# Scores and value products of two heads issued in turn on opposite halves of the array

## The reference

```python
s = einsum('bnqhgd,bnkhd->bnhgqk', qb, kk) * HEAD_DIM**-0.5      # sliding, n = block
s = where(valid, s + bias, NEG); p = softmax(concat([s, sink]))[..., :-1]
o = einsum('bnhgqk,bnkhd->bnqhgd', p, vv)

s = einsum('bqhd,bkhd->bhqk', q[:, q0:q1], k[:, :q1]) * HEAD_DIM**-0.5   # forgetting, block n
s = s + (c[:, :, q0:q1, None] - c[:, :, None, :q1])              # c: cumulative log of the gates
p = softmax(where(valid, s, NEG)); out = einsum('bhqk,bkhd->bqhd', p, v[:, :q1])
merged = sigmoid(ga) * (oa @ w_pa) + sigmoid(gb) * (ob @ w_pb)
```

## Time and profile before

| what | value |
|---|---|
| runs | 1684.04, 1686.79, 1687.28 us; median 1686.79 |
| profiled execution | 1683.52 us, span 1681.3 us from the first to the last instruction |
| granted TensorE clock | 0.994 of full |
| busy: PE, DVE, ACT, POOL | 1633.2, 1341.1, 735.2, 455.5 us |
| sliding steps, to the first forgetting scores | end at 224.83 us |
| first forgetting scores to the first product after the attention loop | 224.83 to 342.67 us |

### The profile page before, as it was taken

One profiled execution on the slowest core, in us unless ns is written; L12 is line 12 of the kernel. 1 busy time (PEld: TensorE's weight loads), 2 busy tenths in 40 slices (PEclk: granted clock), 3 DMA queues, 4 the chain that ended last, 5 costly groups with the idle time before them and its releaser, 6 DMA issues. The chain is left out here.

```text
span 1681.3 us, 26829 instructions
## 1 busy us (share of the span) xinstructions
PE 1633.2 (97%) x9808; PEld 1509.0 (90%) x9808; DVE 1341.1 (80%) x2856; ACT 735.2 (44%) x1288; POOL 455.5 (27%) x314
## 2 busy tenths in 40 slices
PE   5999999999799999999999999999999999999996
PEld 4897776678688899999999999999999999999996
DVE  4534455646568899999999989768899999899898
ACT  3314444443253344667666754444333333333331
POOL 0000000000001023333133342333554555457540
PEclk9999999999899999999999999999999999999998
DMA  4461111023234478899899999999999999999991
GB/s 147 121 198 57 42 50 39 13 84 95 85 99 148 134 251 302 275 353 327 276 311 346 331 347 320 368 406 362 405 404 407 407 409 407 407 407 406 407 404 77
DMA packets 185441, 438.47 MB, mean 261 GB/s; under 512 B 17832, under 2 KB 102000, under 8 KB 182880
## 3 DMA queue, kind: packets, MB, share of 16 engines
q1 hardware_dynamic: 73872, 227.43, 37.1%
q0 software_dynamic: 44080, 161.06, 26.0%
q10 hardware_dynamic: 67360, 48.28, 8.7%
HBM read 380.57 MB, written 56.13 MB: 260 GB/s over the span
## 5 line engine op out<-in xcount | busy, mean ns | idle before, releaser
L469 PE MATMUL psS<-hT_lo,hi 128*128 128x368 f32 (+2 forms) x1464 | 503.1, 344 | 4.6 <-DVE hT_lo L1033 3.9
L460 DVE TENSOR_TENSOR lo<-raw,hi 128x1024 fp32r<-128x1024 f32 x323 | 394.4, 1222 | 132.8 <-ACT hi L456 124.8
L470 PE MATMUL psS<-hT_hi,lo 128*128 128x368 f32 (+2 forms) x1464 | 495.0, 338 | 0.0
L471 PE MATMUL psS<-hT_hi,hi 128*128 128x368 f32 (+2 forms) x1464 | 492.8, 337 | 0.0
L456 ACT ACTIVATE hi<-raw 128x1024 fp32r<-128x1024 f32 x323 | 339.8, 1053 | 160.5 <-PE psS L471 104.0
L578 POOL DMA_INDIRECT gat<-in_u_rows,idx x144 | 216.4, 1503 | 395.9 <-DVE gat L1207 214.6
L469 PEld LDWEIGHTS psS<-hT_lo,hi 128*128 128x128 f32 x1464 | 275.2, 188 | 28.7 <-issue 15.8
L471 PEld LDWEIGHTS psS<-hT_hi,hi 128*128 128x128 f32 x1464 | 275.5, 188 | 12.4
L470 PEld LDWEIGHTS psS<-hT_hi,lo 128*128 128x128 f32 x1464 | 275.2, 188 | 10.1
L578 POOL DMA_INDIRECT gat<-in_v_exp,idx x144 | 222.4, 1544 | 225.5 <-DVE gat L1207 141.6
L773 ACT ACTIVATE act_hi<-act_t 128x368 fp32r<-128x368 f32 x128 | 65.6, 513 | 275.9 <-DVE act_t L1258 265.0
(11 more groups left out here) (314 smaller groups left out, 2667.4 us busy)
## 6 DMA issues: line engine op xcount, KB each, us to landing
raw<-in_u_exp SPq DMA_DIRECT2D x128, 512.0 KB
raw<-in_v_exp SPq DMA_DIRECT2D x128, 512.0 KB
gelu_dram<-gelu ACTq DMA_DIRECT2D x128, 184.0 KB
gates_dram<-gates ACTq DMA_DIRECT2D x92, 256.0 KB
gel_in<-gelu_dram SPq DMA_DIRECT2D x128, 184.0 KB
raw<-in_w_merge SPq DMA_DIRECT2D x24, 512.0 KB
gate_even<-gates_dram SPq DMA_DIRECT2D x8, 1472.0 KB
gate_odd<-gates_dram SPq DMA_DIRECT2D x8, 1472.0 KB
```

The lines of the kernel that those rows point to most:

```text
L460: nc.vector.tensor_tensor(lo[:, n % RING, :], raw[:, n % RING, :], hi[:, n % RING, :].bitcast(F32), ALU.subtract).then_inc(lo_done, 1)
L469: nc.tensor.matmul(out_ap, w_h, x_l, start=start, stop=False)
L470: nc.tensor.matmul(out_ap, w_l, x_h, start=False, stop=False)
L471: return nc.tensor.matmul(out_ap, w_h, x_h, start=False, stop=stop)
```

## The change

Sliding steps now take a head of each key head, so that their two units lie on opposite halves (the host permutes bias and sinks to match). Their scores are not neighbours: the first unit's, one gate tile, a wait on the new semaphore `head_mm` for the first unit's scores, the second unit's. Their value products are issued piece by piece, the units in turn.

Forgetting steps are taken in twos. The scores of steps r and r + 1 (r even) are issued in turn, piece by piece, in iteration r - 1 of PE, after the exponentials of step r - 1; runs of 256 keys or more are cut in two. The values of both are issued in turn in iteration r + 3. `pT` has three buffers in place of two.

```diff
-    tile, half = (h % 4, h // 4) if window else (h // 2, h % 2)
-    return window, n, h, tile, half
+    return window, n, h, h // 2, h % 2
...
+def paired_step(s):
+
+    return len(STEPS[s]) == 1
...
-                    if s >= 3:
-                        act.wait_ge(pv_mm, s - 2)
+                    if s >= 4:
+                        act.wait_ge(pv_mm, s - 3)
...
+            def score_pieces(u):
+
+                pieces = []
+                for c, k0, k1 in key_runs(u):
+                    parts = 2 if k1 - k0 >= 2 * P and not unit_of(u)[0] else 1
...
+            def scores_of_pair(r):
+
+                pe.wait_ge(exp_done, exp_count(r - 1))
+                units = [STEPS[r][0], STEPS[r + 1][0]]
+                if width_of(units[0]) > SEQ:
+                    pe.wait_ge(gate_in_done, N_GATE - 1)
+                pieces = score_pieces(units[0])
+                for a, piece in enumerate(pieces):
+                    for i, u in enumerate(units):
+                        last = score(r + i, u, 0, piece)
+                        if a == len(pieces) - 1:
+                            last.then_inc(s_mm, 1)
...
+            def values_of(parts):
+
+                pieces = pieces_of(parts[0][0])
+                blocks = [0] * len(parts)
+                for a, (_, _, b) in enumerate(pieces):
+                    ends = dict(start=a == 0, stop=a == len(pieces) - 1)
+                    for i, (u, s, first, at_meta) in enumerate(parts):
...
+                            last = mm(dst, vN[:, b, f:f + HD], pT[:, s % 3, at:at + P], **ends)
...
+                if r < N_STEPS and paired_step(r):
+                    if r % 2 == 0:
+                        scores_of_pair(r)
+                    for done in tiles_now:
+                        gate_tile(done)
+                elif r < N_STEPS:
                     if r >= 2:
                         pe.wait_ge(exp_done, exp_count(r - 2))
...
+                    (u0, first0), (u1, first1) = placed(r)
+                    piece, = score_pieces(u0)
+                    score(r, u0, first0, piece).then_inc(head_mm, 1)
+                    for done in tiles_now[:1]:
+                        gate_tile(done)
+                    pe.wait_ge(head_mm, r + 1)
+                    score(r, u1, first1, piece).then_inc(s_mm, 1)
+                    for done in tiles_now[1:]:
+                        gate_tile(done)
...
+                    if not paired_step(s - 2):
+                        u0, u1 = STEPS[s - 2]
+                        second = P * sum(b is not None for _, _, b in pieces_of(u0))
+                        values_of([(u0, s - 2, 0, 0), (u1, s - 2, second, 1)])
+                    elif s % 2 == 1:
+                        values_of([(STEPS[s - 3][0], s - 3, 0, 0), (STEPS[s - 2][0], s - 2, 0, 0)])
```

More of the change, by code:

```diff
@@ L1440, in key_runs, with score @@
                 return runs
+            def score_pieces(u):
+                pieces = []
+                for c, k0, k1 in key_runs(u):
+                    parts = 2 if k1 - k0 >= 2 * P and not unit_of(u)[0] else 1
+                    each = (k1 - k0) // parts
+                    pieces += [(c + i * each, k0 + i * each, k0 + (i + 1) * each) for i in range(parts)]
+                return pieces
+            def score(r, u, first, piece):
+                window, n, h, tile, half = unit_of(u)
+                rows = slice(HD * half, HD * half + HD)
+                q = (qaT if window else qbT)[rows, tile, n * P:(n + 1) * P]
+                c, k0, k1 = piece
+                k = kaT[rows, k0:k1] if window else kbT[rows, tile, k0:k1]
+                return mm(psS[:, r % 2, first + c:first + c + k1 - k0], q, k, start=True, stop=True)
@@ new lines, in gate_tile @@
+            def gate_tile(done):
+                v, k = done // KT, done % KT
+                if k == 0:
+                    pe.wait_ge(lo_done, FIRST_MERGE + v + 1)
+                    if v >= 2:
+                        pe.wait_ge(gate_in_done, v - 1)
+                    if v == N_GATE - 1:
+                        pe.wait_ge(o_hi_done, 2 * NBLK - 1)
+                        pe.wait_ge(o_lo_done, 2 * NBLK - 1)
+                last = slab(FIRST_MERGE + v, (FIRST_MERGE + v) % RING, gate_bank(v), tokens, tokens_lo,
+                            [(k, k)], ends=(k == 0, k == KT - 1))
+                if k == KT - 1:
+                    last.then_inc(slab_used, 1)
@@ new lines, in values_of @@
+            def values_of(parts):
[4 more added lines that the diff above has]
+                    for i, (u, s, first, at_meta) in enumerate(parts):
+                        window, n, h, tile, half = unit_of(u)
+                        w = u // HEADS
+                        if w >= 2 and h == 0 and a == 0:
+                            pe.wait_ge(o_hi_done, w - 1)
+                            pe.wait_ge(o_lo_done, w - 1)
+                        f = half * HD if window else P + h * HD
+                        dst = psO[HD * half:HD * half + HD, w % 2, tile * P:(tile + 1) * P]
+                        if b is None:
+                            slot, at = meta_slot(s, at_meta)
+                            last = mm(dst, vM[:, f:f + HD], pM[:, slot, at, :], **ends)
+                        else:
+                            at = first + blocks[i] * P
+                            last = mm(dst, vN[:, b, f:f + HD], pT[:, s % 3, at:at + P], **ends)
+                            blocks[i] += 1
+                        if a == len(pieces) - 1 and (not window or i == 1):
+                            last.then_inc(pv_mm, 1)
@@ L1443, in _ @@
             for s in range(-1, N_STEPS + 2):
                 r = s + 1
-                if r < N_STEPS:
+                tiles_now = range(tiles_before(max(s, 0)), tiles_before(s + 1))
+                if r < N_STEPS and paired_step(r):
[4 more added lines that the diff above has]
+                elif r < N_STEPS:
                     if r >= 2:
                         pe.wait_ge(exp_done, exp_count(r - 2))
[L1448 to L1470, removed]
+                    (u0, first0), (u1, first1) = placed(r)
```

39 lines of the change are left out of this document (12 added, 27 removed).

## The result

The changed kernel is slower: median 1701.31 us of 4 runs (1698.30 to 1703.63) against 1686.11 of 4 runs of the kernel before on the same chip, a ratio of 1.009 with a 95% interval of 1.0071 to 1.011. Two executions far off the rest, 5558 us of `e7_early_tiles_fill` and 2014 us of the kernel before, are in none of the ratios here. The change costs 15.2 us where 6 was forecast. The time lies inside the stated range of 1685 to 1712 us, but outside the forecast's own of 1688 to 1698. The profiled execution took 1698.30 us, its span 1696.2, 14.9 more than before.

The account below looks back on a forecast made before the run. PE was taken to bound the kernel, busy 1633.2 of 1681.3 us. The terms 5.1 - 9.4 - 18.6 + 28.9 gave +6.0 us on 1683.5, so 1689.5, and 3.3 more for the median: 1693 us, range 1685 to 1712.

Parts of the forecast that it names:

- the wait that the forecast weighed most: Forgetting steps: PE idles before each pair's scores until ACT finishes the exponential of the step just before; sum +28.9 us.
- the m + 1 intervals of term 3: Scores and values on opposite halves: m matmuls of two instructions each take m + 1 start intervals instead of 2m.
- term 3: Overlap of matmuls on opposite halves, in sliding values and in forgetting scores and values: -18.6 us.
- term 4: Forgetting pairs: PE's new wait for the last step's exponential, with slab, block 3 and last-pair additions: +28.9 us.
- Term 1: Sliding steps: gate tile between scores adds shape changes, +6.2 us; grouped values in block 0 save 1.1; sum +5.1.
- Term 2: Forgetting steps: pairing cuts shape changes from 1.36 to 0.77 us a pair; 16 pairs, -9.4 us.
- The upper bound, -28.7: Overlap in scores and values if one half's matmuls lie wholly beside the other's: 28.7 us gained.
- The rival that went with it: Full overlap in scores and values: second head's matmuls cost nothing beside the first's; 1685 us, chance 0.14.
- the tail: End of the forgetting part: the last pair's values wait for their own copy, +1.0 us.
- the second rival: Full overlap in scores and values, -28.7 us, ending below the time before at 1685 us; chance 0.14.

Follow-up runs that it names:

- e7_early_tiles_fill: Changed kernel with early exponentials, four gate tiles moved to steps 36 to 38, and 18 unread transposes before pairs 42 and 44: 1684.27 us, ratio 0.9991.
- e5_filler: Changed kernel with 10, 28, 14, 16 and 12 unread transposes ahead of PE's waits in the last five pairs: 1696.02 us, ratio 1.0055.

## Why the prediction was wrong

The direction was right, and so was the wait that the forecast weighed most. What failed is the size, 15.2 us where 6.0 was forecast, and the step that failed is the one that kept the "full granted clock" for a kernel in which PE waits: the clock had no term, and its fall lengthened PE's work in the loop by 12.6 us. A second step, the m + 1 intervals of term 3, erred the other way by 10.1 us, and term 4 was 4.0 short. That errors of opposite sign left the time inside the stated range is luck, and so in part is the direction: with the overlap and the waits as measured and no fall of the clock, the same sum comes to -0.1.

**Term 1, changes in the sliding steps (+5.1): holds.** In the sliding step above each of the two scores takes 0.63 us to the next start, 0.43 occupied and 0.20 for the change, and the first tile product behind them 0.33, as in the earlier trace rows. With full overlap of the values (-7.0) and the first wait (+2.0) the sliding part should have come to +0.1; it came to +1.3. The missing 1.2 us were not traced.

**Term 2, changes in the forgetting steps (-9.4): not seen by itself, but the part adds up with it** (below).

**Term 3, overlap (-18.6): mis-sized.** The step that failed is "starts keep their order. So m matmuls take m + 1 intervals in place of 2m", with B1 waiting for nothing but A2 still behind A1. The records start in twos 0.007 us apart, so m matmuls take m intervals. The scores of a pair are 0.45, 0.66, 0.88 and 1.19 us by block; less the 0.20 of the change they are half of the 0.48, 0.93, 1.36 and 1.97 of two units one after the other. The upper bound, -28.7, is what these rows give. The forecast also let no weight load of 128 columns come faster than the 0.109 us of the transposes. In the pair at 281.19 of the kernel after the loads of the two heads start 0.035 us apart, those of one head 0.108 or more, so that row was no limit for loads of opposite halves. TensorE: Matmul & The Clock Gate (the Trainium skill, part 3, the mechanism) had said about 4 ns between matmuls on different parts of the array; the trace shows 7 for halves. The rival that went with it had been given 0.14.

**Term 4, the new wait (+28.9): right in mechanism, 4 us short.** The 16 waits are 31.9 us from the earliest possible start, and the tail is 1.04: 32.9. What lacked is in rows above: `oT_hi` between copies and exponential, 0.48 us in five gaps, and the slab of step 37, 3.94 us of wait where 1.7 was counted. The two come to 4.6; what was counted for the others was 0.6 too much.

**The clock: no term at all.** The first paragraph of the prediction noted the "full granted clock" and took it along into a kernel in which PE idles 28.5 us out of 128. PE's work in the low stretches of the loop took 12.6 us longer.

**The sum again.** Forgetting part: -9.4 - 21.7 (the share of 28.7 that is not the sliding values' 7.0) + 30.9 (the waits in it, tail included) + 12.6 = +12.4; measured +10.5. Sliding part +0.1; measured +1.3. Together +12.5 against +11.9. After the loop +3.0: low stretches there sum to 13.7 us against 10.2 before, which is 1.7 of it, and 1.3 stay open. So by this sum the change would have ended near zero without the clock's fall, which is the second rival's place; with it, it ended at 15. That is the lower end, as 12.6 is an upper estimate. From above stand the two runs of `e5_filler` at 0.991 and 0.992: 1690.0 us, 4.3 above the kernel before on the same chip (1685.7, at 0.991 to 0.994). That the clock's fall is a cause was tested directly in block 3; for the other stretches it is read from the windows.

## What to carry to other kernels

Where two steps that shared a double buffer are taken together, the wait for the other engine moves from the step before last to the last one: follow that engine's order from the release to the maximum and further to what is late next, before adding anything up. Interleaving on opposite halves of the array is worth its full half for neighbours of one shape, and is best bought together with the reorder of the other engines (1672.88 against 1701.31 us here). And in a kernel in which PE never idled, price new waits above their length: the granted clock that came down with them made PE's work up to 12.6 us longer, on 32.9 of waits.

## What the hardware showed

- Two float32 matmuls on opposite halves, of rows (scores) or of columns (values), start 0.007 us apart (0.035 in the later twos of scores of 200 columns), and two cost as much as one (scores of block 2: 0.88 us for a pair, 0.87 for one unit in the kernel before).
- Order: unit by unit, the eight score records of a pair still start in twos (0.013 and 0.042 us apart, each two 0.17 to 0.25 after the one before) although the program has the second unit's behind all of the first's. Neighbours of one half with 128 columns or more never stood closer than 0.109 us, and the two records that raise the scores' semaphore, each the last of its unit, are the seventh and the eighth. So the second unit's must have overtaken; the records do not name the half. TensorE: Matmul & The Clock Gate (the Trainium skill, part 3, the mechanism) says that matmuls start strictly in program order. This trace speaks against it.
- Values issued unit by unit did not overtake: 1.88 us against 0.95. A change of shape lies between the units there (16 rows to 128), and they share rows and differ in columns; which of the two holds them back was not tested.
- The granted clock of a part bound by PE stood at 0.50 for 27 of its 128 us once PE had waits in it, first after one of 2.39 us; with PE kept busy it stayed at 1.00 in block 3.
